# Feed-forward of a hybrid decoder trunk: tokens stationary, gate and up columns moving side by side, token tiles staggered at the seams

## The reference, cut to what matters

```python
for i in range(2):
    h = swiglu(rmsnorm(x, g[0]), w_gate[i,0], w_up[i,0], w_down[i,0])
    x = x + 0.5 * rmsnorm(h, g[1])
    h = mixer(rmsnorm(x, g[2]))              # GLA in layer 0, Mamba-2 SSD in layer 1
    x = x + rmsnorm(h, g[3])
    h = swiglu(rmsnorm(x, g[4]), w_gate[i,1], w_up[i,1], w_down[i,1])
    x = x + 0.5 * rmsnorm(h, g[5])
# swiglu(h) = (silu(h @ w_gate) * (h @ w_up)) @ w_down     w_gate, w_up: 1024 x 2816, w_down: 2816 x 1024
# rmsnorm(x, g) = x * rsqrt(mean(x*x) + 1e-6) * g
```

## Time and profile before

| | us |
|---|---|
| median of three runs | 1246.89 (1246.22 to 1247.04) |
| profiled execution, first to last instruction (span) | 1245.1 |
| PE busy | 1160.8 |
| DVE busy | 826.2 |
| ACT busy | 651.8 |

### The profile page before, as it was taken

How to read it: one execution, slowest core, us unless ns; L and a number is a source line. 1 busy time by engine, 2 the same in 40 slices (tenths; PEclk the granted TensorE clock), 3 DMA queues, 4 the chain that set the end, 5 groups by cost and what they waited for, 6 DMA issues and landing times.

```text
span 1245.1 us, 18895 instructions
## 1 busy us (share of the span) xinstructions
PE 1160.8 (93%) x6792; PEld 988.2 (79%) x6792; DVE 826.2 (66%) x1228; ACT 651.8 (52%) x907; POOL 76.1 (6%) x85
## 2 busy tenths in 40 slices
PE   5999998989979999999999997999999977999996
PEld 4888886888758888877888886788888856888885
DVE  4756567665656565566665657799998984756564
ACT  4554545554336555655656554554555423655653
POOL 5000001000010000001000001221111111000000
PEclk8999999999989999999999998999999978999999
DMA  8655555264225655553655554254445411655541
GB/s 261 206 181 190 188 183 169 81 219 139 70 100 169 201 177 194 198 173 101 213 192 190 181 168 136 86 182 139 135 139 163 154 50 51 200 182 192 187 150 68
DMA packets 162062, 197.93 MB, mean 159 GB/s; under 512 B 6212, under 2 KB 145568, under 8 KB 162032
## 3 DMA queue, kind: packets, MB, share of 16 engines
q1 hardware_dynamic: 159936, 190.86, 47.3%
q0 software_dynamic: 2096, 6.67, 1.7%
HBM read 196.46 MB, written 1.05 MB: 159 GB/s over the span
## 4 chain that ended last, share of the span: by engine, by line
PE 81%; DVE 11%; ACT 4%; issue 2%; DMA 1%; DVEq 0%; ACTq 0%; POOLq 0%
PE ps L1113 26%; PE ps L1162 23%; PE ps L1115 13%; PE ps L1125 8%; PE ps L1135 6%; DVE ws L724 2%; ACT ws L468 2%; DVE scr L784 1%; PE ps L1178 1%; PE ps L1403 1%; PE ps L1379 1%; ACT scr L490 1%; DVE xres L774 1%; DVE scr L769 1%; DMA gpre<-in_norm_gain 1%
## 5 line engine op out<-in xcount | busy, mean ns | idle before, releaser
L724 DVE TENSOR_TENSOR ws<-raw,ws 128x1024 fp32r<-128x1024 f32 (+1 forms) x224 | 419.3, 1872 | 243.3 <-ACT ws L468 243.3
L1113 PE MATMUL ps<-xT,ws 128*128 128x512 f32 x1408 | 501.2, 400 | 5.8 <-DVE ws L724 3.8
L1115 PE MATMUL ps<-xT,ws 128*128 128x256 f32 x1408 | 396.2, 281 | 0.0
L468 ACT ACTIVATE ws<-raw 128x2048 fp32r<-128x2048 f32 x180 | 342.5, 1909 | 79.6 <-PE ps L1162 75.7
L1162 PE MATMUL ps<-ws,hT 128*128 128x512 f32 x1344 | 322.1, 396 | 6.3 <-DVE hT L969 3.9
L1113 PEld LDWEIGHTS ps<-xT,ws 128*128 128x128 f32 x1408 | 265.9, 189 | 72.4 <-issue 4.0
L1162 PEld LDWEIGHTS ps<-ws,hT 128*128 128x128 f32 x1344 | 251.0, 190 | 63.4 <-issue 5.4
L1115 PEld LDWEIGHTS ps<-xT,ws 128*128 128x128 f32 x1408 | 267.1, 190 | 1.6
L474 ACT ACTIVATE lo<-ps 128x256 f32<-128x256 f32 x176 | 66.2, 378 | 162.9 <-PE ps L1115 162.9
L1125 PE MATMUL ps<-xT,ws 128*128 128x256 f32 x960 | 119.2, 284 | 0.1
L1125 PEld LDWEIGHTS ps<-xT,ws 128*128 128x128 f32 x960 | 116.5, 192 | 0.7 <-issue 0.7
(11 more groups left out here) (185 smaller groups left out, 704.0 us busy)
## 6 DMA issues: line engine op xcount, KB each, us to landing
raw<-in_ffn_w_gate SPq DMA_DIRECT2D x88, 512.0 KB, 4.6
raw<-in_ffn_w_up SPq DMA_DIRECT2D x88, 512.0 KB, 4.7
raw<-in_ffn_w_down SPq DMA_DIRECT2D x88, 512.0 KB, 4.0
raw<-in_ssd_w_in SPq DMA_DIRECT2D x48, 512.0 KB, 4.7
raw<-in_gla_w_in SPq DMA_DIRECT2D x24, 512.0 KB, 4.8
raw<-in_ssd_w_out SPq DMA_DIRECT2D x16, 512.0 KB, 4.2
raw<-in_gla_w_out SPq DMA_DIRECT2D x8, 512.0 KB, 4.5
gpre<-in_norm_gain POOLq DMA_DIRECT2D x6, 512.0 KB, 5.1
```

The source lines that it names most:

```text
L468: act.activation(ws[:, slot, 0, :], raw[:, slot, :], ACT.Copy).then_inc(hi_done[slot], 1)
L724: return dve.tensor_tensor(ws[:, slot, 1, cols], raw[:, slot, cols], ws[:, slot, 0, cols].bitcast(F32), ALU.subtract)
L1113: pe.matmul(bank, ws[:, slot, 0, off:off + P], xT[:, k, :, :].rearrange("p a t -> p (a t)"), start=(k == 0), stop=False, skip_group_check= ...
L1115: mm = pe.matmul(bank[:, 0:T], ws[:, slot, 1, off:off + P], xT[:, k, 0, :], start=False, stop=(k == KD - 1), skip_group_check=True)
```

## The change

Feed-forward units now keep the tokens stationary. For each step k over the features and each of the two token tiles t, three matmuls of 512 columns are issued: 256 gate columns and 256 up columns from slots 0 and 1 move side by side into bank A+t. The result has tokens on partitions, so the pre-norm's inverse root (one number for a token) is applied to the products: as the scale of silu (on ScalarE) and in the product with up (on VectorE). The pre-norm gain (one number for a feature) is applied when the transposed x is split, as a scale of the copy. The hidden values are transposed on TensorE (`hidden_T`, four transposes a unit) and split from PSUM into `hT`, which has two buffers now. Gate and up weights are split in four quarters, each of two steps k and both slots, behind the sweep that reads them. Down weights alternate between slots 2 and 3.

At the seams the two token tiles are staggered: the last output of tile 0 is finished first and normed while TensorE still works on tile 1. In front of a feed-forward the raw x is transposed; in front of a mixer it is still scaled first. Norm operations come in pieces of 512 columns. The zero matmuls are left out, except one round before each mixer. GpSimd has no gain product any more, and the gains come by one small load and a transpose. In GLA one projection (P2, gates) moves into the seam.

```diff
-KEEP_WARM = 3
-SLOT_GATE, SLOT_UP, SLOT_DOWN = 0, 1, 2
+SLOT_DOWN = 2, 3
+NQ = 4
+QW = UNIT // NQ
...
# SyncE
+            def load_gate_up(wg, wu, u, unit, h):
+                ks = slice(h * KD // 2, (h + 1) * KD // 2)
+                sp.wait_ge(gu_lo, unit * 4 + (2 * h - 2))
+                col = at(u * UW)
+                for slot, w in ((0, wg), (1, wu)):
+                    dst = raw[:, slot, :].rearrange("p (k n) -> p k n", k=KD)
+                    sp.dma_start(dst[:, ks, :], cols(w, col)[:, ks, :]).then_inc(gu_loaded[h], 16)
...
+            sp.dma_start(xres[:, 0, :], x[0, 0:P, :]).then_inc(x_in[0], 16)
+            for q in range(NQ):
+                quarter(ffn_w_gate[0, 0], 0, q)
+                quarter(ffn_w_up[0, 0], 1, q)
+                if q == 0:
+                    sp.dma_start(xres[:, 1, :], x[0, P:2 * P, :]).then_inc(x_in[1], 16)
...
# ScalarE
+            def x_high(b, t, ks):
+                for k in ks:
+                    act.wait_ge(xnT, 8 * b + 4 * t + k // 2 + 1)
+                    act.activation(xT[:, k, 0, t * P:(t + 1) * P], ps[:, A + k // 2, (k % 2) * P:(k % 2 + 1) * P],
+                                   ACT.Copy, scale=gcol[:, 16 * b + k:16 * b + k + 1]).then_inc(xT_hi, 1)
...
+            def boundary(b):
+                mixed = b < NPH and PHASES[b][0] != "ffn"
...
+                post_square(b, 0, 0)
+                post_square(b, 0, 1)
+                post_root(b, 0)
+                if PHASES[b - 1][0] == "ffn":
+                    hT_high(gate_units_before(b) - 1, 1, 0)
+                if mixed:
+                    pre_root(b, 0)
+                post_square(b, 1, 0)
+                if mixed:
+                    post_square(b, 1, 1)
+                    post_root(b, 1)
+                    x_high(b, 0, range(KD))
+                    pre_root(b, 1)
...
+                    x_high(b, 1, range(KD))
+                    return
+                if b < NPH:
+                    x_high(b, 0, range(KD // 2))
+                post_square(b, 1, 1)
+                post_root(b, 1)
+                if b < NPH:
+                    x_high(b, 0, range(KD // 2, KD))
+                    pre_root(b, 0)
+                    x_high(b, 1, range(KD))
+                    pre_root(b, 1)
...
# ScalarE, feed-forward unit (VectorE has the same order with lo, hidden and hT_low)
+                def body(u, unit, down, par, bank=A):
+                    hi(*down)
+                    for q in range(2):
+                        gate_up_hi(unit + 1, q)
+                    if bank == A:
+                        gate_up_hi(unit + 1, 2)
                     for t in range(NT):
+                        gate(unit, t, bank)
...
+                    hT_high(unit, 0, par)
+                    gate_up_hi(unit + 1, 3)
+                    hT_high(unit, 1, par)
...
# end of a feed-forward in front of a mixer
+                    first_hi(ph + 1, SLOT_P1)
+                    first_hi(ph + 1, SLOT_P2)
...
# VectorE
+            def hidden(unit, t, bank):
+                dve.wait_ge(silu_g, unit * 2 + t + 1)
+                dve.scalar_tensor_tensor(out=fm[:, 2 + t, :], in0=ps[:, bank + t, UW:2 * UW], scalar=RPRE[t], in1=fm[:, t, :],
+                                         op0=ALU.mult, op1=ALU.mult).then_inc(h_done, 1)
...
# VectorE's boundary in front of a mixer
+                gained(b, 0, 0)
+                gained(b, 0, 1)
+                post_root(b, 0)
...
+                x_update(b, 0, 0)
+                x_update(b, 0, 1)
+                gained(b, 1, 0)
+                if mixed:
+                    pre_root(b, 0)
+                    x_scaled(b, 0)
+                    gained(b, 1, 1)
+                    post_root(b, 1)
+                    x_update(b, 1, 0)
+                    x_update(b, 1, 1)
+                    x_low(b, 0, range(KD))
+                    pre_root(b, 1)
+                    x_scaled(b, 1)
...
+                    x_low(b, 1, range(KD))
+                    return
...
# TensorE
+            def gate_up(k, t, bank):
+                for a, b in ((0, 0), (0, 1), (1, 0)):
+                    mm = pe.matmul(ps[:, bank + t, :].rearrange("p (s n) -> p s n", s=2), xT[:, k, a, t * P:(t + 1) * P],
+                                   ws[:, 0:2, b, k * UW:(k + 1) * UW], start=(k == 0 and a + b == 0),
+                                   stop=(k == KD - 1 and a == 1), skip_group_check=True)
+                return mm
...
+                def body(u, unit, slot, count, par):
+                    sweep(unit, u)
+                    first = isinstance(u, int) and u == 1
+                    for t in range(NT):
+                        down_ready(unit - 1, t, slot, count)
+                        down_half(slot, par, t, 0, first)
+                        hidden_T(unit, t)
+                        down_half(slot, par, t, 1, first)
...
+                sweep(last, NF - 1)
+                down_ready(last - 1, 0, *odd)
+                down_half(odd[0], 1, 0, 0)
+                hidden_T(last, 0)
+                down_half(odd[0], 1, 0, 1)
+                hidden_T(last, 1)
+                down_ready(last, 0, *even)
+                down_half(even[0], 0, 0, 0, last=True)
+                down_half(even[0], 0, 0, 1, last=True)
+                down_ready(last - 1, 1, *odd)
+                down_half(odd[0], 1, 1, 0)
+                down_half(odd[0], 1, 1, 1)
+                down_ready(last, 1, *even)
+                down_half(even[0], 0, 1, 0, last=True)
+                if ph + 1 < NPH and PHASES[ph + 1][0] == "ffn":
+                    x_transposed(ph + 1, 0)
+                down_half(even[0], 0, 1, 1, last=True)
...
             def gla_start(ph, n0):
+                def gates(t):
+                    split(SLOT_P2, n0[SLOT_P2])
+                    token_tiles(SLOT_P2, 0, (t,))
+                both_transposed(ph, gates)
...
# last groups of a mixer
-                    if outp and proj or last:
-                        add_output()
+                    if outp and proj:
+                        add_output(g - 2)
+                    elif last:
+                        add_output(n - 1, (0,), True)
+                        add_output(n - 2, (1,))
+                        add_output(n - 1, (1,), True)
...
                     if scan and not proj:
-                        add_output()
+                        add_output(n - 2, (0,))
```

More of the change, by code:

```diff
@@ L84, in ffns_before, with mixers_before, gate_units_before, down_use @@
     return sum(PHASES[q][0] == "ffn" for q in range(phase))
+def mixers_before(phase):
+    return sum(PHASES[q][0] != "ffn" for q in range(phase))
+def gate_units_before(phase):
+    return NF * ffns_before(phase)
+def down_use(u):
+    return SLOT_DOWN[u % 2], u // 2
 def pipeline(eng, n, body):
@@ L191, in trunk @@
         A, B, C, E = 4, 5, 6, 7
-        CW0, CB0 = 0, 0
         GG0, GS0, GB0 = 32, 40, 56
@@ L710, in _ @@
                     mixer(ph, kind, SSD_G)
-                norm(ph + 1)
+                boundary(ph + 1)
         @block.vector
@@ L725, in low_part @@
                                          ALU.subtract)
-            def sums(low, count, banks, outs, done, tiles=(0, 1)):
-                for c in tiles:
-                    dve.wait_ge(low, count + c + 1)
-                    dve.tensor_tensor(outs[c], ps[:, banks + c, 0:T], lo2[:, c, :], ALU.add).then_inc(done, 1)
             def rsqrt2(ss, width):
@@ new lines, in ffn, with body @@
+            def ffn(ph):
+                units = gate_units_before(ph)
+                n0 = [used_before(ph, s) for s in range(4)]
+                for t in range(NT):
+                    dve.wait_ge(r_done, NT * ph + t + 1)
+                def body(u, unit, down, par, bank=A):
+                    lo(*down)
+                    for q in range(2):
+                        gate_up_lo(unit + 1, q)
+                    if bank == A:
+                        gate_up_lo(unit + 1, 2)
+                    for t in range(NT):
+                        hidden(unit, t, bank)
+                    if bank != A:
+                        gate_up_lo(unit + 1, 2)
+                    hT_low(unit, 0, par)
+                    gate_up_lo(unit + 1, 3)
+                    hT_low(unit, 1, par)
+                body(0, units, (SLOT_DOWN[0], n0[SLOT_DOWN[0]]), 0, 0)
+                body(1, units + 1, (SLOT_DOWN[1], n0[SLOT_DOWN[1]]), 1)
+                with dve.Fori(1, NF // 2) as i:
+                    for c in range(2):
+                        body(i * 2 + c, i * 2 + (units + c), (SLOT_DOWN[c], i + n0[SLOT_DOWN[c]]), c)
+                last = units + NF - 1
+                lo(SLOT_DOWN[0], NF // 2 + n0[SLOT_DOWN[0]])
+                same = ph + 1 < NPH and PHASES[ph + 1][0] == "ffn"
+                if same:
+                    for q in range(3):
+                        gate_up_lo(last + 1, q)
+                for t in range(NT):
+                    hidden(last, t, A)
+                hT_low(last, 0, 0)
```

(48 more changed lines are left out.)

635 lines of the change are left out of this document (347 added, 288 removed).

## The result

The changed kernel takes 1255.9 us (median; 1252.0 to 1257.6), the kernel before 1246.6 on the same chip: ratio 1.0072, 95% interval 1.0054 to 1.0089. It is slower by 9, where 17 less was forecast. Its profiled execution took 1252.0, with a span of 1250.2 (before 1245.1). It is the shortest of its four runs, so the profile shows 5 of the 9 us.

What follows compares the result with a forecast made beforehand. PE, busy 93% of the span, was taken as the bound, with holes at the seams. Terms 9 - 10.8 - 15 + 8 - 5 - 3.6 = -17.4 on the 1245.1 us span gave a median of 1229 us, range 1209 to 1248.

Steps and rivals of the forecast that it cites:

- T: At a feed-forward to feed-forward seam: the end of the phase's last sweep, with both down groups still to do.
- quarter 3 is done at 15 and asked for at 25: Steady unit, us from the start of a sweep: the last quarter of the next gate/up weights is split well before PE needs it.
- start: Kernel start, first loads and first two sweeps: -5 us, bounds 0 and -9; second sweep waits for loads and hidden values.
- feed-forward to feed-forward: The seam between two feed-forward phases: -10.8 us; -13 if the norm chain is wholly hidden, -5 if the second tile's shows whole.
- GLA to feed-forward: First of the two seams out of a mixer: -7.5 us each, -15 together; bounds -4 and -11 each.
- SSD to feed-forward: Second of the two seams out of a mixer: -7.5 us, by the same steps; bounds -4 and -11.
- The unit: One steady feed-forward unit on PE: 17.0 us instead of 16.79, +0.2, or +9 us over 44 units.
- Rival C: Gate/up sweep slower per matmul through its two-piece moving operand; 1266 at the bound of two matmuls of 256; chance 0.13.
- Seams into a mixer: Feed-forward to GLA and to SSD: +4 us each, from splits ahead of the norm operations and a colder clock; bounds -3 and +8.
- rival A: Seams before the mixers gain too, -3 each instead of +4, and the unit is 16.93: 1212 us; chance 0.18.
- End: From the last matmuls to the end of the span: 5.8 us instead of 9.4, -3.6.
- Rival B: Seams close less than counted, small steps wait for other engines and the tiles' chains run in a row: 1242, end 1256; chance 0.19.

Runs made afterwards that it cites:

- e5: e4 plus, in each phase's second unit, activations and hidden product ahead of the third unit's quarter 2 on ScalarE and VectorE; 1223.9 us, ratio 0.9824.
- e7: Changed kernel with gate and up as separate matmuls of 256 columns; 1279.1 us, ratio 1.027.
- e6: e4 with the splits of the mixer's first tiles moved from ahead of the boundary's small norm operations to between them; 1227.8 us, ratio 0.986.
- e9: e5 plus e6's move of the splits at the mixer seams; 1216.1 us, ratio 0.9753.
- e10: e9 plus 16 zero products of 512 columns on PE at each of the two seams into a mixer; 1210.9 us, ratio 0.9717.
- e11: e5 without the stagger of the token tiles: each phase's last down products in one order for both tiles; 1231.3 us, ratio 0.9884.
- e1: Changed kernel with quarters 0 and 1 of each feed-forward's second unit split ahead of the first unit's down weights; 1244.6 us, ratio 0.999.
- e8: e2 plus e5's move of activations and product, without early quarters 0 and 1 and with SyncE's order unchanged; 1234.1 us, ratio 0.9905.
- a0: The changed kernel measured again as it is, beside the kernel before; 1254.1 us, ratio 1.0074.
- e2: Changed kernel with quarter 3 of each feed-forward's second unit split ahead of the first unit's hT copy; 1239.4 us, ratio 0.9939.
- e3: Changed kernel with both edits, e1's and e2's; 1244.0 us, ratio 0.9983.
- e4: e3 plus SyncE issuing the first half of the third unit's gate and up columns ahead of its down rows; 1232.7 us, ratio 0.9904.

## Why the prediction was wrong

**The step that failed** is the one that carried the seams: "Then the next unit's quarter 0 is late: down split on ScalarE and VectorE (T + 25.6) comes ahead of it, so it is ready at T + 26.8." I found this wait and priced it at 2.4; it was 3.0, and in two of the three phases the matmuls behind it took 1.6 more at the low clock. And there I stopped: from the next unit on I used the order of time of the steady unit, in which "quarter 3 is done at 15 and asked for at 25". At the second unit of a phase it is not done early. It stands behind a high part of hT that comes out of the middle of the next sweep, the load for unit 2 stands behind it, and unit 1's product behind that load's quarter. This costs 9.4 to 9.7 in each of three phases and 4.0 in the first, 33 in all. When it is taken away (e5) the stretches are: start -5.2 (forecast -5), feed-forward to feed-forward -11.6 (-10.8), GLA to feed-forward -8.7 and SSD to feed-forward -8.1 (-7.5 each). The terms themselves were near, for a kernel with another order in three queues. The whole kernel gained 30 by it and not 33: in the profile of e5 the stretch over GLA took 4 us more than in the changed kernel's.

**The unit** was mis-sized: +0.2 and +9 over 44 units forecast, +0.08 and some +3 measured. Matmuls step by 0.227 with the two-piece operand, below the 0.229 that I took from down, and four transposes cost 0.44 (two pairs of 0.22), at the low end of 0.43 to 0.62; I took 17.0 where the low end was 16.93. The sum also had a part of this twice, since the terms of the seams were already reckoned with the new unit's steps: from the third sweep of a phase on, where the table counts it, 17.0 a unit would give +5 and not +9. "I am wrong if units come faster than 16.8": they came at 16.87. Rival C is excluded. (Its own end was short by 2: 2112 matmuls at 0.248 for 0.229 are 39, not 37.) What it feared is there when the product really is made as two: 13 ns a matmul (e7).

**Seams into a mixer.** +8 forecast, +9 measured, right in size and in most of its reasons. The wait for hT's low part (2.2 twice) and the low clock (0.71 and 0.69 in the two windows from 208 to 224, before GLA; 0.50 from 764 to 772, before SSD) came as said, and P1's wait for its split (4.1) too. As e6 and e9 show, 5 to 8 us could be had there by moving the splits that stood ahead of the norm's operations, and as e10 shows another 5 by holding the clock, most of it before GLA (4.6 in the profiles). So rival A is wrong for this kernel: these seams did not gain.

**Start.** -1.2 for -5. The transfer that ends last there was foreseen, its place was not: the second sweep waited 0.9 and the hidden product behind it 3.8. **End:** -3.4 for -3.6; e11 shows that the stagger gives it.

**Rival B** has the time that came out (its end was 1256), but not the reason. Its small norm steps are not what cost most: PE's wait for the scaled x fell from 23.5 to 6.6, and e1, which touches no norm step, gave back 9.4. That the time fell on B's end is chance: B had the seams out of a mixer at -4 each, and they came at +0.5 and +1.5. "If any load ends the wait in the units" was among the signs that I named for being wrong, and that is the sign that came, in the third unit.

Left open: what sets the clock in the stretch over GLA. Its code is the same in the changed kernel, e1 to e5, e7 and e8, and it takes 165.7 to 170.3.

## What to carry to other kernels

Where a steady rhythm is written out by hand, follow the first two or three turns by themselves, on every in-order queue, that of SyncE included: what the steady order puts ahead with 10 us to spare can stand ahead of the one thing that is late at the start. Take the stalls away one after the other and look at what grows: two moves that were each right gave less together (10) than one alone (15) until the third queue was put in order. A stall can also have a second price, in the clock of the matmuls behind it, and it is not paid each time: read it from several stalls before you put it in a sum.

## What the runs showed of the hardware

- What a wait costs in clock is not settled by its length. The wait of 3.0 us for quarter 0 comes twelve times in the profiles of the changed kernel, a0, e2 and e8: the 24 matmuls behind it took 7.2 us seven times (granted clock 0.76 from 376.71 to 383.89) and the usual 5.6 five times (1.00 from 1061.88 to 1067.40). In the waits for the hidden product, 12 matmuls took 4.0 to 5.3 for the usual 2.8 after all sixteen of 3.6 to 5.6 us (the changed kernel, a0, e1, e3), after five of the twelve of 1.6 to 3.0 (e2, e4, e6), and after none of the twenty of 0.5 to 0.8 (e5, e8 to e11).
- The clock in a seam is not settled by the code there. With the same wait of 2.25 before them, the 24 matmuls at the end of the seam before GLA took 3.12 us in the changed kernel and 4.62 in e5:

```profile
225.00 3.12 PE L1355 MATMUL ps<-ws,xT 128*128 128x256 f32 x24 [2.25 <-DVE xT L898]
```

```profile
221.50 4.62 PE L1371 MATMUL ps<-ws,xT 128*128 128x256 f32 x24 [2.25 <-DVE xT L907]
```

- 16 products of zeros in front of GLA held the granted clock at 1.00 where it was 0.57 and 0.79, in stretches where the transposes ran in both kernels. The rule of the Trainium skill that the prediction weighed (TensorE: Matmul & The Clock Gate, Part 4: PE-mode transpose) fits this, but no run tells transposes from the idle time around them.
- A moving operand in two pieces of 256 columns from slots far apart costs no more than one of 512: 0.227 against 0.229. As two matmuls they cost 13 ns more for each one added in the steady unit (17.50 for 16.87).
- A piece of 512 KB took 4.8 to 5.0 us from its issue when 1 MB was under way, and 7.3 (379.99 to 387.28) with 3 MB issued within 3.7 us.
